# A reordered beginning: four one-k units, half token tiles of the norm between them, and unit 0's parts on VectorE

## The reference

```python
h = rmsnorm(x, attn_norm_g[l])
proj = jnp.einsum('bsd,de->bse', h, w_in[l])
qa, ka, va, qb, kb, vb = jnp.split(proj, split_pts, axis=-1)
```

## Time and profile before

| | us |
|---|---|
| runs of the kernel | 992.17, 993.47, 994.43 |
| median | 993.47 |
| span of the profiled execution | 994.2 |
| TensorE busy in it | 975.9 (98%) |
| VectorE, ScalarE, GpSimd busy | 715.9, 522.4, 58.4 |

### The profile page before, as it was taken

The page is one execution under the profiler, slowest core; times in us unless marked ns, Lnnn a source line. Parts: engine busy times, 40 slices in busy tenths (PEclk is TensorE's granted clock), DMA queues, the critical chain, the costliest instruction groups (busy, mean ns, idle before and its releaser), DMA issues.

```text
span 994.2 us, 12848 instructions
## 1 busy us (share of the span) xinstructions
PE 975.9 (98%) x4770; PEld 806.2 (81%) x4770; DVE 715.9 (72%) x1074; ACT 522.4 (53%) x808; POOL 58.4 (6%) x62
## 2 busy tenths in 40 slices
PE   8999999999999999999999999999999999999998
PEld 6878788888887888888878888877888878888886
DVE  5867778886786767767869988686667766566653
ACT  6576565554346444444467645567454474443531
POOL 3310100000000000000000022021000000000000
PEclk9998999999999999999999999999999999999999
DMA  7940667888795777778756766865565737664761
GB/s 245 300 132 1 222 221 226 279 271 274 264 316 192 254 262 246 247 251 325 262 149 208 229 210 190 288 194 175 150 199 199 236 111 222 215 209 134 253 225 51
DMA packets 116444, 214.64 MB, mean 216 GB/s; under 512 B 9058, under 2 KB 16506, under 8 KB 116126
## 3 DMA queue, kind: packets, MB, share of 16 engines
q1 hardware_dynamic: 116238, 213.73, 65.7%
q10 hardware_dynamic: 144, 0.10, 0.0%
HBM read 212.71 MB, written 2.13 MB: 216 GB/s over the span
## 4 chain that ended last, share of the span: by engine, by line
PE 89%; DVE 5%; DMA 2%; ACT 2%; issue 1%; POOL 0%; SPq 0%; ACTq 0%; DVEq 0%
PE ps L1179 27%; PE ps L1181 26%; PE ps L1180 26%; PE ps L1229 3%; PE ps L1316 2%; DVE wlo L1846 2%; PE ps L1271 1%; PE ps L1297 1%; PE ps L1207 1%; ACT whi L1484 1%; DMA raw<-in_w_up 1%; DMA raw<-in_w_in 1%; DMA araw<-in_w_ada 1%; DMA raw<-in_ffn_w_in 1%; PE ps L1367 1%
## 5 line engine op out<-in xcount | busy, mean ns | idle before, releaser
L1484 ACT ACTIVATE whi<-raw 128x1024 fp32r<-128x1024 f32 (+2 forms) x307 | 313.0, 1028 | 282.4 <-PE ps L1181 193.0
L1846 DVE TENSOR_TENSOR wlo<-raw,whi 128x1024 fp32r<-128x1024 f32 (+2 forms) x307 | 358.3, 1189 | 49.0 <-ACT whi L1484 48.2
L1179 PE MATMUL ps<-whi,hTh 128*128 128x512 f32 (+1 forms) x832 | 326.2, 392 | 2.7 <-DVE wlo L1846 2.7
L1181 PE MATMUL ps<-whi,hTl 128*128 128x512 f32 (+1 forms) x832 | 316.5, 380 | 0.0
L1180 PE MATMUL ps<-wlo,hTh 128*128 128x512 f32 (+1 forms) x832 | 316.4, 380 | 0.0
L1179 PEld LDWEIGHTS ps<-whi,hTh 128*128 128x128 f32 x832 | 156.8, 188 | 33.6 <-DVE wlo L1846 3.8
L1181 PEld LDWEIGHTS ps<-whi,hTl 128*128 128x128 f32 x832 | 156.7, 188 | 30.8
L1180 PEld LDWEIGHTS ps<-wlo,hTh 128*128 128x128 f32 x832 | 157.0, 189 | 26.9 <-issue 0.2
L2188 DVE SCALAR_TENSOR_TENSOR aacc<-araw,cs,aacc 128x512 f32<-128x512 f32 x126 | 94.4, 749 | 4.8 <-DMA araw<-in_w_ada 2.2
L2430 POOL TENSOR_TENSOR stat<-stat,mhalf 128x8 f32<-128x8 f32 (+3 forms) x29 | 38.3, 1331 | 632.3 <-DVE stat L1862 486.3
L1179 PE MATMUL ps<-whi,uh_ffn 128*128 128x512 f32 x176 | 69.8, 396 | 0.0
(11 more groups left out here) (251 smaller groups left out, 1092.0 us busy)
## 6 DMA issues: line engine op xcount, KB each, us to landing
raw<-in_ffn_w_in SPq DMA_DIRECT2D x80, 512.0 KB, 4.5
araw<-in_w_ada SPq DMA_DIRECT2D x72, 512.0 KB, 4.9
raw<-in_w_mix SPq DMA_DIRECT2D x64, 512.0 KB, 4.4
raw<-in_ffn_w_out SPq DMA_DIRECT2D x44, 512.0 KB, 4.9
raw<-in_w_up SPq DMA_DIRECT2D x32, 512.0 KB, 4.9
raw<-in_w_down SPq DMA_DIRECT2D x32, 512.0 KB, 5.2
raw<-in_w_out SPq DMA_DIRECT2D x16, 512.0 KB, 4.2
raw<-in_w_in SPq DMA_DIRECT2D x12, 512.0 KB, 5.6
```

The source lines that it names most:

```text
L1179: pe.e.matmul(o, ah, h[:, j, :], start=s0, stop=False, skip_group_check=True)
L1181: r = pe.e.matmul(o, al, h[:, j, :], start=False, stop=s1, skip_group_check=True)
L1484: act.e.activation(uflat(whi, u), uflat(raw, u), ACT.Copy).then_inc(hi.up(u), 1)
L1846: v.tensor_tensor(uflat(wlo, u), uflat(raw, u), uflat(whi, u).bitcast(f32), SUB).then_inc(lo_dve.up(u), 1)
```

## The change

The beginning is written out in a function of its own, `begin()`:

- qa's first four units are all worked at the beginning, in the order 0(t0), 1(t0), 2(t0), 0(t1), 1(t1), 2(t1), 3(t0), 3(t1), and the four half token tiles of the norm stand between them in the order (0,0), (1,0), (0,1), (1,1).
- After the first transposes, TensorE makes six more products of `ones` ("fill"), as at the very start.
- Unit 0's upper part is a cast on VectorE and not on ScalarE; its two parts stand ahead of the first split.
- The first split is in groups of one, one and two k; that of (1, 0) is one group of four.
- Limits: unit 4's upper part behind turn(1,1), no limit from half(3,1) on. Squares, means and setup come behind half(3,1).
- SyncE issues x(0,0), units 0 to 2, x(1,0), unit 3, x(0,1), x(1,1), units 4 to 7, and the rest as before.

```diff
+        def begin():
+            first = blocks["qa"]["units"][:FIRST]
+            pairs.take("qa")
+            hold(0)
+            upper_of(0)
+            lower_of(0)
+            turn_half("attn", 0, 0)
+            order.append(("fill",))
+            split("attn", 0, 0)
+            for u in (1, 2):
+                upper_of(u)
+                lower_of(u)
+            upper_of(3)
+            half(0, 0)
+            turn_half("attn", 1, 0)
+            split("attn", 1, 0)
+            lower_of(3)
+            half(1, 0)
+            turn_half("attn", 0, 1)
+            split("attn", 0, 1)
+            half(2, 0)
+            half(0, 1)
+            turn_half("attn", 1, 1)
+            split("attn", 1, 1)
+            hold(1)
+            advance()
+            half(1, 1)
+            half(2, 1)
+            half(3, 0)
+            hold(None)
+            half(3, 1)
+            assert first == [0, 1, 2, 3]
+            sums("attn")
+            for t in range(2):
+                order.append(("scale", "attn", t))
+            order.append(("setup", "rope"))
...
-        hold(0)
-        turn("attn", 0, LAG["attn", "between0"], LAG["attn", "behind0"])
-        head("attn", "qa")
-        gemm("qa", skip=LAG["attn", "first"])
+        begin()
+        gemm("qa", skip=FIRST)
...
+    def split_groups(stage, t, p):
+        if p:
+            return ((0, 4),)
+        if stage == "attn":
+            return ((0, 4),) if t else ((0, 1), (1, 1), (2, 2))
+        return ((0, 2), (2, 2))
...
+        def products_of_ones():
+            for _ in range(6):
+                pe.e.matmul(ps[7][:, 0:128], ones[:, 0:128], ones[:, 0:128], start=True, stop=True)
...
         def prep(u):
+            if u == 0:
+                return
             act.wait_ge(*ld_raw[slot(raw, u)](u))
...
         def prep(u):
-            dve.wait_ge(*hi(u))
+            if u == 0:
+                dve.wait_ge(*ld_raw[slot(raw, u)](u))
+                step(v.tensor_copy(uflat(whi, u), uflat(raw, u)))
+                dve.wait_ge(*dve_step.now())
+            else:
+                dve.wait_ge(*hi(u))
...
+        load_x(0, 0)
+        for u in range(3):
+            load_unit(u)
+        load_x(1, 0)
+        load_unit(3)
+        load_x(0, 1)
+        load_x(1, 1)
+        for u in range(4, 2 * NR):
+            load_unit(u)
```

More of the change, by code:

```diff
@@ L16 @@
 KU = 2
+FIRST = 4
 NEVER = (None, 0)
-LAG = {("attn", "behind0"): 3, ("attn", "between0"): 0, ("attn", "between1"): 4, ("attn", "first"): 2,
-       ("attn", "hold1"): 0, ("attn", "turn1"): 0, ("attn_a", "wait"): 17, ("attn_as", "round"): 19,
+LAG = {("attn_a", "wait"): 17, ("attn_as", "round"): 19,
        ("attn_as", "wait"): 1, ("attn_as", 0): 3, ("attn_as", 1): 16, ("attn_as", 2): 23, ("attn_as", 3): 7,
@@ L365, in build @@
     for key, c0, n in (("qa", 0, 512), ("ka", 512, 256), ("qb", 768, 512), ("kb", 1280, 512), ("vb", 1792, 512)):
-        block(key, "w_in", 0, 8, c0, n, "attn", small=4 * (key == "qa"))
+        block(key, "w_in", 0, 8, c0, n, "attn", small=FIRST * (key == "qa"))
     for c in range(2):
@@ L529, in split, with turn_half @@
             order.append(("split", stage, t, p))
+        def turn_half(stage, t, p):
+            misc.take("norm", stage, t, p)
+            misc.drop("norm", stage, t, p)
+            sqr.take("n", stage, t, p)
+            sqr.drop("n", stage, t, p)
+            order.append(("turn", stage, t, p))
         def turn(stage, t, between=0, behind=None, late=False):
             for p in range(2):
[L533 to L537, removed]
+                turn_half(stage, t, p)
                 if not (p and late):
@@ L541, in turn, with upper_of, lower_of @@
                 advance()
+        def upper_of(u):
+            assert u == at["prep"]
+            order.append(("hi", u))
+            at["prep"] += 1
+        def lower_of(u):
+            order.append(("lo", u))
+        def begin():
[34 more added lines that the diff above has]
+            order.append(("setup", "rope"))
         def ada():
@@ L726, in head @@
         def head(stage, then):
-            first = blocks[then]["units"][:LAG["attn", "first"] if stage == "attn" else LEAD]
+            first = blocks[then]["units"][:LEAD]
             assert LAG[stage, "turn1"] < len(first)
@@ L738, in head @@
                 tick()
[L739 to L743, removed]
             at["quiet"] = False
@@ L1061, in build, with split_ends @@
     HT_FREE = {"attn": None, "mlp": "vb", "ffn1": "up7", "mix": "ffn1b5", "merged": "gb1", "ffn2": "wob1"}
+    def split_groups(stage, t, p):
[4 more added lines that the diff above has]
+        return ((0, 2), (2, 2))
+    def split_ends(stage, t):
+        return [4 * p + c + n - 1 for p in range(2) for c, n in split_groups(stage, t, p)]
     def left_ready(act, k, t):
@@ L1076, in left_ready @@
             return lower(f"{act[2:]}g{k // 4}", p)
-        return lower(act, t, 3 if k > 3 else k // 2)
+        return lower(act, t, next(e for e in split_ends(act, t) if e >= k))
     def hT_free(act, t=1):
@@ L1188, in gate_mm @@
             for t in range(2):
-                pe.wait_ge(*lower("mix", t, 3))
+                pe.wait_ge(*lower("mix", t, 7))
             for k in range(8):
@@ L1455, in tensor_program @@
                 jobs[f"{m}g{i}"] = glu_job(f"{m}g{i}", (n + 255) // 256)
+        def products_of_ones():
+            for _ in range(6):
+                pe.e.matmul(ps[7][:, 0:128], ones[:, 0:128], ones[:, 0:128], start=True, stop=True)
         pe.wait_ge(*made_ident("ones"))
-        for _ in range(6):
-            pe.e.matmul(ps[7][:, 0:128], ones[:, 0:128], ones[:, 0:128], start=True, stop=True)
+        products_of_ones()
         for name in ("attn_a", "attn_b", "fx0", "fx1"):
@@ L1471, in tensor_program @@
                 turn(*of)
+            elif what == "fill":
+                products_of_ones()
             elif what == "gate_mm":
@@ L1876, in split @@
             dve.wait_ge(*hT_free(stage, t))
-            for c, n in ((0, 2), (2, 2)) if p == 0 else ((0, 4),):
+            for c, n in split_groups(stage, t, p):
                 k = 4 * p + c
@@ L1883, in split @@
                 v.tensor_tensor(hTl[:, k:k + n, ts], s, hTh[:, k:k + n, ts].bitcast(f32), SUB).then_inc(
-                    lower.up(stage, t, (k + n - 1) // 2), 1)
-                sqr.give(lower(stage, t, (k + n - 1) // 2), "n", stage, t, p)
+                    lower.up(stage, t, k + n - 1), 1)
+                sqr.give(lower(stage, t, k + n - 1), "n", stage, t, p)
         def setup(part):
@@ L2615, in store, with load_x @@
                             x[t][:, c * 512:(c + 1) * 512]).then_inc(st_out.up(t, c), 16)
[L2617 to L2622, removed]
+        def load_x(t, c):
+            q.dma_start(x[t][:, c * 512:(c + 1) * 512],
+                        d["x"][0, t * 128:(t + 1) * 128, c * 512:(c + 1) * 512]).then_inc(ld_x[t][c].up(), 16)
+        load_x(0, 0)
[7 more added lines that the diff above has]
+            load_unit(u)
         q.dma_start(rope[:, :, :, :], d["rope"]).then_inc(ld_rope.up(), 16)
```

## The result

| | before | changed |
|---|---|---|
| median us, 22 runs each | 994.38 | 997.09 |
| lowest to highest | 991.53 to 996.85 | 994.67 to 1000.61 |
| ratio | | 1.0027 (1.0018 to 1.0036) |
| span of the profiled execution | 994.2 | 994.7 |
| TensorE starts unit 5 | 19.30 | 21.29 |

The account below looks back on a forecast made before the run. TensorE, busy 98% of the span, was taken as the bound, with unit 5's start setting the end. Its move from 19.30 to 21.7 us added 2.4 to the median 993.47, giving 995.9, range 992.6 to 998.6.

Parts of the forecast that it names:

- Which wait ends last: Beginning: the start of unit 5 on TensorE, 19.30 before, moves the end; the first matmul's 1.5 us gain does not.
- Landings by place: Load queue: place in the queue decides landing; unit 3 at 8.7 us, x(0,1) at 9.4.
- ScalarE's order: Beginning: turn(1,1) late at 12.95, then four uppers ahead of the squares, which begin at 16.9 instead of 14.48.
- the sum: Whole kernel: unit 5 at 21.7 instead of 19.30, +2.4 us on the median, 995.9; chance 0.42.
- the 4.82 us from the first square to unit 5: Beginning: four squares, mean, constants and unit 5's lower half, priced from before's trace as 19.30 - 14.48.
- rival B: TensorE's new hole at 19.3 to 21.7: low clock behind it adds 1.7 us, +4.1 in all, 997.6; chance 0.28.
- Unit 4's gate (C): Squares off the path, unit 4's lower half late at 16.6: unit 5 at 19.3, 993.5; chance 0.21 together with E.
- TensorE's own order (D): Beginning without both waits: unit 5 at 18.2, -1.1 us, 992.4; chance 0.09.
- What the forecast put at nothing: Six extra products of ones before the first half unit: 1.3 to 2.8 us, ending at 6.3, nothing on the chain moves.

Follow-up runs that it names:

- three groups: Changed kernel with the split of (1,0) in groups of one, one and two k instead of one group of four; 998.60 us, ratio 1.0042.
- all repairs: Changed kernel with late means, unit 4 early and three groups together, the extra products of ones kept; 994.50 us, ratio 1.0005.
- loads-only kernel: Kernel before with the changed order of loads and nothing else; 996.34 us, ratio 1.0025.
- the squares first: Changed kernel with the limit lifted behind the squares, so the uppers of units 5 to 7 follow them on ScalarE; 995.85 us, ratio 1.0016.
- no fill: Changed kernel without the six extra products of ones; 995.40 us, ratio 1.0010.
- unit 0 on ScalarE: Changed kernel with unit 0's upper half made on ScalarE again instead of by a VectorE cast; 997.54 us, ratio 1.0036.
- late means: Changed kernel with means and setup behind the lower halves of units 5 to 7 on VectorE, ScalarE's order untouched; 995.65 us, ratio 1.0012.
- unit 4 early: Late means, plus unit 4's upper and lower half made ahead of turn(1,1) and its split; 993.51 us, ratio 0.9993.
- changed again: Changed kernel run again with no edit, beside others on one chip; 997.69 us, ratio 1.0037.

## Why the prediction came out as it did

**Which wait ends last.** Right. The first matmul came 0.6 and 1.6 us earlier in the two profiles and the kernel became slower. In all thirteen profiles TensorE's instructions at 80 us are shifted against before by what unit 5 is, to 0.3 us. The margin in before is thin: without the wait TensorE's own order would have had unit 5 at 19.07 (the product before it starts at 18.84, and one takes 0.23), 0.2 earlier. On one chip the repairs that move unit 5 (21.47 to 19.86, 19.16 and 18.14) move the median down in that order (997.69, 995.85, 995.65, 993.51). But the end does not simply move by the same: three groups (unit 5 at 20.04, median 998.60) and all repairs (16.91, 994.50) fall out of that order. In the profiles the shift changes most between 80 and 335 us, by the clock and by the hole that is looked at below.

**Landings by place.** Right to 0.4 us: unit 3 landed at 8.6 (predicted 8.7), x(0,1) in the loads-only kernel at 9.0 (9.35).

**ScalarE's order.** Right in each step of the chain. Predicted and measured: wait of half(0,1) to 11.6, 11.51; turn(1,1) on ScalarE 12.95, 12.95; squares 16.9, 16.90; unit 4 at 16.6, 16.60. Off the chain the extra products took nearly their upper price (4.90 to 7.32 where 6.3 was taken), and cost nothing there.

**Unit 5 and the sum.** 21.7 predicted, 21.29 measured: the term that was too large is the 4.82 us from the first square to unit 5, which took 4.39. Nearly all of it is behind the mean: the constants and the lower half took 1.79 from mean to matmul instead of 2.18, while first square to mean took 2.60 instead of 2.64. In before's trace GpSimd's products of the rotation table ran until 20 us beside that piece; that they slowed it is argued, and the runs don't settle it: with the squares first they also ran beside unit 5's lower half, and it took 1.24 there against 1.43 in before. So the beginning is worth +2.0 to +2.2, not +2.4, and the median moved by 2.7 and, in the second series, by 3.8. That the forecast of +2.4 came so near to 2.7 is in part luck: a term 0.4 too large stands against 0.5 us or more from behind the beginning, which the sum had at nothing. (The profiled span is 0.7 above the median of the three runs, not 0.8; nothing rests on it.)

**The clock in the new hole (rival B).** Did not show. Five profiles have the hole of 1.6 to 1.8 us (changed, again, no fill, three groups, unit 0 on ScalarE) and in none does a low stretch follow it; filling it brought nothing. The hole is also shorter than the 2.4 us which the forecast compared with the two of before. Where the clock falls is the attention stage: after its hole of 2.3 us the granted clock is 0.50 for 3.4 us or twice that in 11 of the 14 profiles, between 80 and 93 us, and not there with late means, with all repairs and with unit 0 on ScalarE (in the last it falls at 121.7). The start varies too. In the ten profiles with extra products the clock record begins at full clock between 4.35 and 7.39 (4.35 and 7.39 are the same kernel), and the clock stays up until the attention stage or longer; in the four without it begins at 4.97 (and falls at 8.39), 5.64, 9.77 and 13.88. That the same kernel starts differently from one execution to the next is in step with the Trainium skill, TensorE: Matmul & The Clock Gate, Part 1, whose rule is that what is counted runs free of the kernel's start. The same page advises, for products with few rows (section "HAM oscillation — how this bites in real kernels"), to arrange the work so that TensorE stays at full clock. Here that found no gain: with the extra products the kernel before kept its clock from 8.39 to 11.80, and TensorE then waited 1.13 us for the split.

**Unit 4's gate (C) and TensorE's own order (D).** Both were worked out for a kernel without the gate in front of them, and the runs made these kernels: 19.3 predicted for C, 19.16 measured with late means; 18.2 for D, 18.14 with unit 4 early. They did not happen in the changed kernel because the squares are late there. Of the two conditions that the forecast names for C neither is enough by itself, as its own count against C (unit 5 at 20.1) says: with half(0,1) on time unit 5 was at 20.04, with the squares earlier at 19.86.

**What the forecast put at nothing** is the extra products. Three pairs speak against that, each by its ratio to before on its own chip: changed again 1.0037 against 1.0010 without them; all repairs 1.0005 against 0.9993; the kernel before 1.0007 against 1 by definition. The differences are 0.0027, 0.0012 and 0.0007, each uncertain by 0.0010 to 0.0016 (my estimate from the intervals): the first is clear of that, the others aren't; all have one sign, and the beginnings' timelines explain at most 0.4 us of the first. Uneven draws of the clock don't explain it either: unit 0 on ScalarE and the kernel without extra products ran on one chip with the same mean granted clock (0.9974 and 0.9975) and 2.1 us apart (997.54 and 995.40), with unit 5 only 0.4 apart; and the kernel before with extra products was slower than without at a higher mean clock (0.9977 against 0.9965).

The place where the profiles differ can be found by following ScalarE's instructions through before and before with extra products: the latter is 2.14 us ahead at 300 us (0.4 from the beginning, the rest from one low stretch of clock instead of two at 84 us), 1.54 ahead at 306, 0.15 ahead at 331 and the same at 977. In all thirteen profiles the shift against before is at the end less than 0.5 us from what it is at 335 us. What happens between 300 and 331 begins with a hole of TensorE at 308 us (start of the first gated feed-forward), long behind the change (waits ended by DVE W):

```profile
311.06 1.06 PE L1207 MATMUL ps<-ident,W 128*128 128x128 f32 x8 [1.32 <-DVE W L1870]
```

for before, and with late means

```profile
309.14 1.07 PE L1264 MATMUL ps<-ident,W 128*128 128x128 f32 x8 [2.56 <-DVE W L1939]
```

In the four profiles without the extra products it is 1.18 to 1.44, in the ten with them 1.12 to 2.56 (mean 1.9); where it reached 1.9 the clock fell behind it in three of six. It also varies within one kernel: 1.38 and 2.12 in the two profiles of the changed one. Behind it stands the landing of a weight load, 5.20 us after issue in before and 6.31 with late means. I have no mechanism by which products at 5 us would reach 308 us, and one profile of each kernel is one draw. Whether the extra products cost 1 to 2 us by way of this hole, or these are uneven draws of landings, stays open. Open is also the three-group kernel's 998.60: its granted clock was low on average (0.9953 over its six runs, against 0.9964 for the changed kernel again), which by the slope below is worth only 0.5 to 0.7 us.

## What to carry to other kernels

An early start of the bound engine was worth nothing here, because a small step that nobody is in a hurry for (four squares and two means) stood in front of a needed one on a helper engine's queue: find the last wait in the chain, and order each engine's queue by due time. When a limit on preparation is lifted at one point, count what is appended there ahead of the next step in line. And before believing a microsecond between two profiles, follow single instructions through both: here the shift was 2.0 us for 60 us and then hidden by the clock. Profile the same kernel twice before believing a detail of its start: the first half unit was at 7.32 in one profile and at 6.38 in the other.

## What the runs showed of the hardware

- Loads of 256 KB issued 0.45 us apart landed in order of issue: moving x(0,1) from second to seventh place moved its landing from 4.6 to 9.0 us.
- A low stretch of 3.4 us, at 1.2 GHz, cost TensorE 1.55 us in the attention stage (between the two profiles above). At 8 us, beside ScalarE's chain, its removal brought no gain that the runs could tell. Over the runs of before on three chips the time rises by 0.5 to 0.66 us for each 0.001 by which the mean granted clock is lower, and the number of low stretches differs between executions of one kernel.
- Splitting 512 columns in steps of 128, 128 and 256 on VectorE cost 0.22 to 0.23 us for a 128-wide cast and 0.29 for a 128-wide difference, against the 0.22 and 0.3 taken in the forecast.
